# Opening of a hybrid encoder layer: the first head's fourth projection summed chunk by chunk between the modulation's weight pieces

## The chip, the cores and the metric

The kernel runs on one core of one Trainium2 chip. The metric is the device time of one execution in microseconds (us), as the median of several runs. A profiled execution gives the engines' timelines: TensorE (PE; its weight loads are PEld), VectorE (DVE), ScalarE (ACT), GpSimd (POOL), SyncE (SP, which issues most DMAs).

## The reference

One layer over two requests of 256 tokens each, model width 2048, all in float32. Only the start matters here:

```
mod = silu(c) @ ada_w + ada_b                    # 2048 x 12288
sh1, sc1, g1, sh2, sc2, g2 = split(mod, 6)
h = rmsnorm(x, mix_pre_w) * (1 + sc1) + sh1      # 512 tokens x 2048
proj = h @ w_in                                  # per head: k, q, dk, dq (4 x 128 columns), then values and gate
... 8 heads of retention and of differential attention, w_out, gate, norm
... second modulation, and a product-key expert layer (PEER) over 16384 experts
```

## The kernel before

**Arithmetic.** A float32 product is made of three fp32r matmuls over a high and a low part of each operand (`split_products`, L854 to L859: high x high, high x low, low x high). The high part of a weight block is a rounding copy by ScalarE (`split_high`, L1424), the low part the difference (GpSimd in the opening, `first_low`, L2519; VectorE in the heads, `head_low`, L2038). Below, a "product" is such a triple over one chunk of 128 rows of h.

**The opening** computes shift and scale of the first modulation and forms h, transposed, in 16 chunks of 128 x 512. The weights `ada_w` come in 32 pieces of 1 MB, four to a block of two chunks. SyncE loads them in order into a ring of five places (`ada_load`, L499; a piece waits for `ada_done` of the one that held its place). Places 3 and 4 of the ring also move: pieces 28 and 29 go to `ada_late`, because `w_fourth` lies over ring places 3 and 4 (`ada_place`, L465). TensorE takes the pieces in its loop over p (from L875): `ada_piece(p)` (L836), then at p % 4 == 3 `row_columns` (L844), which turns the block's sums into columns; ScalarE and VectorE then modulate the block's even and odd chunk, and GpSimd and VectorE make their low parts.

**Products between the pieces.** `chunk_order` (L116) writes a list by hand: the products of projections 0, 1 and 2 of head 0 over chunks 0 to 11, at most two to a step, a chunk not before step 4 * (k // 2) + 6 and a projection not before `W_READY` (its weights' split). Of the steps from 10 on, 17, 21, 25, 29, 30 and 31 hold none. After the last piece the remaining products of the three follow (chunk 13, 12, then 15 and 14 in each). Then `head_step(0, None)` runs `project(0, 3)`, the fourth, as one closed run of 16 products out of `w_fourth`, and `project(0, 4)` to `project(0, 7)`, values and gate in quarters (128x384 matmuls). Then head 1 begins with `project(1, 0)`.

**The weights of the projections** come in pieces through `w_raw`, two places in turn (`piece_load`, L508; waits until the piece two before is split). Piece 2 goes to `w_third`, piece 3 to `w_fourth`. Piece 3 is loaded after the last `ada_w` piece, split high by ScalarE after block 7, and its low part is shared: first half GpSimd, second half VectorE, which counts it on `h_odd`; the load of piece 5 waits for that.

**ScalarE's order in `head_step(0, None)`:** evacuate projections 0, 1, 2 (`evacuate`, L1444, L1453), split pieces 4 and 5, evacuate 3, split 6, 7 and 8 (8 is head 1's first), with a wait on `proj` each. **VectorE's order:** late piece 0, low part of 4, late 1, low 5, late 2 to 4, low 6, late 5 to 7, low 7, late 8 to 10, low 8, late 11. A "late piece" (`late_piece`, L2023 and L2027) is a row-wise product and sum for the later parts of the modulation, two passes over 128x1024, whose loads (`col_load`, L519) wait for a place in a ring of four. SyncE issues the loads of pieces 5 to 8 between those column loads (`head_loads`, L534).

Of the kernel before, what the change touches and what calls it, by code (L numbers as in the profile page):

```python
# [22 lines left out]
P = 128  # L23
D = 2048
KD = D // P
# [15 lines left out]
ADA_FULL = 25  # L41
# [70 lines left out]
W_READY = (7, 8, 11)  # L112
# [3 lines left out]
def chunk_order():  # L116

    queue = sorted((max(W_READY[n], 4 * (k // 2) + 6), k // 2, 1 - k % 2, n, k) for n in range(len(W_READY)) for k in range(KD - 4))
    slots = []
    for p in range(ADA_PIECES):  # L120
        slots.append([queue.pop(0)[3:] for _ in range(2) if queue and queue[0][0] <= p])
    assert not queue
    return slots


CHUNKS = chunk_order()
# [57 lines left out]
def build_program(nc, x, ct, c_rows, ada_w, ada_wt, ada_b, rows, w_t, w_v, w_o, w_q, keys_t, decay, lams, post1, pre2, post2,  # L184
# [9 lines left out]
    with ExitStack() as ctx:  # L194
# [264 lines left out]
        def ada_slot(n):  # L459
            return n % ADA_RING if n < ADA_FULL else (0, 1, 2, 3, 4, 0, 1)[n - ADA_FULL]  # L460

# [3 lines left out]
        def ada_place(n):  # L465
            return ada_late[n - ADA_FULL - 3] if n in (ADA_FULL + 3, ADA_FULL + 4) else ada_ring[ada_slot(n)]

# [24 lines left out]
        def _(sp):  # L492
# [6 lines left out]
            def ada_load(n):  # L499

                if n == ADA_FULL + 3:
                    sp.wait_ge(S["xtr"], KD)
                wait(sp, "ada_done", max([m for m in range(n) if ada_slot(m) == ada_slot(n)], default=-1) + 1)
                sp.dma_start(ada_place(n), ada_w[n]).then_inc(S[f"ada_in{ada_slot(n)}"], 16)
# [3 lines left out]
            def piece_load(h, n):  # L508

                wait(sp, "w_low", 8 * h + n - 1)  # L510
                if isinstance(h, int) and h == 0 and n == 5:
                    sp.wait_ge(S["h_odd"], BLOCKS + 1)
# [42 lines left out]
            for n in range(ADA_PIECES):  # L555
# [7 lines left out]
                if n == 8:  # L563
                    piece_load(0, 2)
                if n == LOG_PIECE:
# [3 lines left out]
            piece_load(0, 3)  # L569
            sp.wait_ge(S["silu_out"], 16)  # L570

            sp.wait_ge(S["ada_done"], ADA_FULL + 5)
# [5 lines left out]
            piece_load(0, 4)  # L578
# [246 lines left out]
        def _(pe):  # L825
# [35 lines left out]
            def chunk_product(n, k):  # L861
# [4 lines left out]
                high, low = (w_third[:, 0, c], w_third[:, 1, c]) if n == 2 else (w_high[:, n, c], w_low[:, n, c])  # L866
                last = split_products(bank(n), ((high, low), (h_hi[:, k, :], h_lo[:, k, :])), k == 1, k == KD - 2)
# [22 lines left out]
            for n, k in ((1, KD - 3), (2, KD - 3), (0, KD - 4), (1, KD - 4), (2, KD - 4)):  # L890
                chunk_product(n, k)
            for n in range(3):
# [3 lines left out]
            def project(h, n):  # L896
                wait(pe, "w_low", 8 * h + n + 1)
                r = n % 2
                place = own_place(h, n)
                high, low = (place[:, 0, :], place[:, 1, :]) if place is not None else (w_high[:, r, :], w_low[:, r, :])  # L900
                if place is not None:
                    pe.wait_ge(S["h_odd"], BLOCKS + 1)
# [90 lines left out]
            def head_step(h, a):  # L993

                def p(n):
                    if h is not None and not (a is None and n < 3):
# [392 lines left out]
        def _(act):  # L1389
# [34 lines left out]
            def split_high(h, n):  # L1424
# [4 lines left out]
                if own_place(h, n) is not None:  # L1429
                    act.wait_ge(S["xtr"], KD)  # L1430
                    if n == 3:
                        act.wait_ge(S["ada_done"], ADA_FULL)
# [11 lines left out]
            def evacuate(h, n):  # L1444
# [4 lines left out]
                if n < 4:  # L1449
# [3 lines left out]
                    acti(dst, bank(n), ACT.Copy, scale=P ** -0.5 if n == 0 else 1.0).then_inc(S["proj_ev"], 1)  # L1453
# [85 lines left out]
            for j in range(BLOCKS):  # L1539
# [5 lines left out]
                if j == 1:  # L1545
                    split_high(0, 2)
                if j == LOG_BLOCK + 1:
# [5 lines left out]
            split_high(0, 3)  # L1553
# [257 lines left out]
        def _(dve):  # L1811
# [118 lines left out]
            for j in range(1, BLOCKS):  # L1930
# [8 lines left out]
            dve.wait_ge(S["w_high"], 4)  # L1939
            vec.tensor_tensor(w_fourth[:, 1, WT // 2:], w_raw[:, 1, WT // 2:], w_fourth[:, 0, WT // 2:].bitcast(f32), ALU.subtract)\  # L1940
                .then_inc(S["h_odd"], 1)

# [106 lines left out]
            def head_step(h, a, link, last=False):  # L2049
# [22 lines left out]
                if a is None:  # L2072
                    late(0)
                    low(4)
                    late(1)
                    low(5)
                    late(2, 3, 4)
# [440 lines left out]
        def _(pool):  # L2518
            def first_low(n):  # L2519
# [3 lines left out]
                w = WT // 2 if n == 3 else WT  # L2523
                nc.gpsimd.tensor_tensor(low[:, 0:w], w_raw[:, n % 2, 0:w], high[:, 0:w].bitcast(f32), ALU.subtract)\
# [14 lines left out]
            first_low(3)  # L2539
# [181 lines left out]
```

## Time and profile before

| | us |
|---|---|
| median of 3 runs | 3203.61 (3201.92 to 3204.26) |
| the profiled execution | 3205.48 |
| its span (first to last instruction) | 3203.7 |
| TensorE matmul busy, whole span | 3139.6 |
| the last `ada_w` piece begins on TensorE | 106.87 |
| `project(0, 3)` begins, `project(0, 4)` begins | 117.63, 128.64 |
| head 1 begins | 162.42 |

In a timeline a row is: start, length, engine, line, operation, tiles written and read, shape, count of merged instructions, and in brackets the idle time before it with what ended it. A matmul's length is from its start to its modelled end, and matmuls overlap: the start of the next is what tells the pace. An issue's last number is the time until the data had landed.

### The profile page before, as it was taken

To read this page: it belongs to the slowest core of one execution; us is meant where nothing else is said; L and a number is where in the kernel's file an instruction comes from. 1 tells how busy PE (TensorE), PEld (TensorE's weight loads), DVE (VectorE), ACT (ScalarE), POOL (GpSimd) and SP (SyncE) were. 2 spreads that over 40 slices of the span, in tenths; PEclk is the share of its full clock that TensorE was granted. 3 is DMA by queue.
4 is the path that set the end of the run, shared out by engine and by line. 5 is a ranking of instruction groups with operands and counts; after the bars stand their busy time and mean duration, and the time that the engine had idled before them with its cause. 6 is when DMAs were issued, how large, how long until landed. Compare 5 with 4: busy or idle time off the path is not lost. (4 is left out here: it accounts for less than half of the span.)

```text
span 3203.7 us, 49077 instructions
## 1 busy us (share of the span) xinstructions
PE 3139.6 (98%) x19669; PEld 2984.7 (93%) x19669; DVE 2732.5 (85%) x3945; ACT 1115.8 (35%) x1457; POOL 894.6 (28%) x570
## 2 busy tenths in 40 slices
PE   7999999999999999999999999999999999999998
PEld 3788888888998888999999999999999999999998
DVE  4688888888888999979888898888688888888888
ACT  2223322333224456943333332332332332332333
POOL 2100000002445781022333233332223333333331
PEclk9999999999999999999999999999999999999999
DMA  9844444444657413899999999999799999999997
GB/s 388 322 174 165 167 168 170 162 166 172 222 184 263 158 54 122 232 332 375 376 362 378 376 379 368 366 377 357 314 374 366 357 364 360 378 362 373 369 360 299
DMA packets 175730, 929.95 MB, mean 290 GB/s; under 512 B 17025, under 2 KB 50998, under 8 KB 80310
## 3 DMA queue, kind: packets, MB, share of 16 engines
q1 hardware_dynamic: 124278, 554.01, 47.0%
q0 software_dynamic: 51264, 373.32, 30.0%
q8 instruction: 132, 2.16, 0.3%
q14 instruction: 56, 0.46, 0.0%
HBM read 891.80 MB, written 34.55 MB: 289 GB/s over the span
## 5 line engine op out<-in xcount | busy, mean ns | idle before, releaser
L1657 ACT ACTIVATE sb_raw_hi<-sb_raw_ring 128x2048 fp32r<-128x2048 f32 x256 | 491.2, 1919 | 1121.9 <-DMA sb_raw_ring<-in_v_t 574.5
L1207 PE MATMUL ps_all<-sb_h_lo,sb_raw_hi 128*128 128x336 f32 x2048 | 638.3, 319 | 0.0
L2275 DVE TENSOR_TENSOR sb_raw_lo<-sb_raw_ring,sb_raw_hi 128x2048 fp32r<-128x2048 f32 x255 | 585.1, 2295 | 52.4 <-ACT sb_raw_hi L1657 51.9
L1207 PE MATMUL ps_all<-sb_h_hi,sb_raw_hi 128*128 128x336 f32 x2016 | 628.6, 319 | 0.0
L1270 PE MATMUL ps_all<-sb_w_hi,sb_raw_hi 128*128 128x336 f32 x2032 | 623.3, 316 | 5.3 <-ACT sb_raw_hi L1657 2.2
L1271 PE MATMUL ps_all<-sb_w_lo,sb_raw_hi 128*128 128x336 f32 x2032 | 622.7, 315 | 0.0
L2637 POOL DMA_INDIRECT sb_gather_ring<-in_u_tab,sb_kept x178 | 277.3, 1558 | 758.8 <-DVE sb_kept L2419 563.8
L2637 POOL DMA_INDIRECT sb_gather_ring<-in_v_tab,sb_kept x178 | 300.7, 1689 | 609.0 <-DVE sb_acc_a L2432 384.6
L1270 PEld LDWEIGHTS ps_all<-sb_w_hi,sb_raw_hi 128*128 128x128 f32 x2032 | 382.3, 188 | 6.6 <-issue 3.8
L1207 PEld LDWEIGHTS ps_all<-sb_h_lo,sb_raw_hi 128*128 128x128 f32 x2048 | 387.3, 189 | 0.0
L1271 PEld LDWEIGHTS ps_all<-sb_w_lo,sb_raw_hi 128*128 128x128 f32 x2032 | 381.9, 188 | 0.0
L1207 PEld LDWEIGHTS ps_all<-sb_h_hi,sb_raw_hi 128*128 128x128 f32 x2016 | 380.5, 189 | 0.0
L1214 PE MATMUL ps_all<-sb_h_hi,sb_raw_lo 128*128 128x336 f32 x2016 | 337.5, 317 | 2.3 <-DVE sb_raw_lo L2275 2.3
L1284 PE MATMUL ps_all<-sb_w_hi,sb_raw_lo 128*128 128x336 f32 x2032 | 333.7, 316 | 0.0
L2419 DVE CUSTOM_DVE_ANT_0 sb_gather_ring<-sb_gather_ring,sb_arena 128x2048 f32<-128x2048 f32 x128 | 291.5, 2288 | 31.7 <-DMA sb_gather_ring<-in_u_tab,sb_kept 31.5
L2432 DVE SCALAR_TENSOR_TENSOR sb_acc_a<-sb_gather_ring,sb_kept,sb_acc_a 128x2048 f32<-128x2048 f32 x127 | 298.2, 2348 | 22.1 <-DMA sb_gather_ring<-in_v_tab,sb_kept 18.9
L1214 PEld LDWEIGHTS ps_all<-sb_h_hi,sb_raw_lo 128*128 128x128 f32 x2016 | 314.2, 188 | 2.8 <-DVE sb_raw_lo L2275 2.8
L1284 PEld LDWEIGHTS ps_all<-sb_w_hi,sb_raw_lo 128*128 128x128 f32 x2032 | 316.8, 188 | 0.0
L2546 POOL TENSOR_TENSOR sb_w_low<-sb_w_raw,sb_w_high 128x1024 fp32r<-128x1024 f32 (+1 forms) x36 | 90.8, 2545 | 746.7 <-ACT sb_w_high L1564 746.7
L1436 ACT ACTIVATE sb_w_high<-sb_w_raw 128x1536 fp32r<-128x1536 f32 (+1 forms) x62 | 105.0, 1695 | 370.4 <-PE ps_all L859 367.1
L857 PE MATMUL ps_all<-sb_h_hi,sb_w_high 128*128 128x512 f32 x480 | 192.0, 400 | 2.1 <-DVE sb_h_lo L1892 1.7
L858 PE MATMUL ps_all<-sb_h_lo,sb_w_high 128*128 128x512 f32 x480 | 187.4, 390 | 0.0
(346 smaller groups left out, 5547.5 us busy)
## 6 DMA issues: line engine op xcount, KB each, us to landing
sb_raw_ring<-in_u_t SPq DMA_DIRECT2D x128, 1024.0 KB
sb_raw_ring<-in_v_t SPq DMA_DIRECT2D x128, 1024.0 KB
sb_arena<-in_ada_wt SPq DMA_DIRECT2D x94, 512.0 KB, 6.1
sb_w_raw<-in_w_t SPq DMA_DIRECT2D x32, 1024.0 KB, 4.9
sb_small<-in_ada_w SPq DMA_DIRECT2D x30, 1024.0 KB, 10.8
sb_w_raw<-in_w_v SPq DMA_DIRECT2D x32, 768.0 KB, 4.3
sb_g_ring<-table_scratch SPq DMA_DIRECT2D x30, 672.0 KB
table_scratch<-sb_stage SPq DMA_DIRECT2D x7, 2688.0 KB, 12.3
```

Source lines behind the costliest of these rows:

```text
L857: mm(b, a_hi, b_hi, start=start, stop=False)
L858: mm(b, a_hi, b_lo, start=False, stop=False)
L1207: last = mm(acc, raw_hi[:, r[0], kk * P:(kk + 1) * P], part, start=i == 0, stop=False)
L1214: last = mm(acc, raw_lo[:, place, kk * P:(kk + 1) * P], high_of(k, kk), start=False, stop=kk == KD - 1)
L1270: mm(accs[c], v, w_hi[:, slots[e], :], start=e == 0, stop=False)
L1271: return mm(accs[c], v, w_lo[:, slots[e], :], start=False, stop=False)
L1284: last = mm(accs[c], raw_lo[:, place, e * VW + c * P:e * VW + (c + 1) * P], w_hi[:, slots[e], :], start=False, stop=e == S8 - 1)
L1657: acti(raw_hi[:, k % 2, :], raw_ring[:, k % RAW, :], ACT.Copy).then_inc(S["un_hi"], 1)
L2275: vec.tensor_tensor(raw_lo[:, k % RAW, :], raw_ring[:, k % RAW, :], raw_hi[:, k % 2, :].bitcast(f32), ALU.subtract)\
L2419: vec.tensor_tensor_reduce(out=ring, in0=ring, in1=h2a if kind == "own" else h2x[rows, :], scale=1.0, scalar=0.0, op0=ALU.mult, op1=ALU.ad ...
L2432: vec.scalar_tensor_tensor(acc, ring, hid_all[rows, c:c + 1], acc, ALU.mult, ALU.add).then_inc(S["gr_used"], 1)
L2637: pool.indirect_dma_start(out=gather_ring[:, n % GRING, :], out_offset=None, in_=u_tab if n < DOTS else v_tab, in_offset=bass.IndirectOffs ...
```

## The change

The fourth projection of head 0 is summed chunk by chunk like the other three. `chunk_order` keeps the list of the first three as it is and fills steps that hold fewer than two products with those of projection 3, from step 20 on; four are left and returned as `CHUNKS_LEFT`, and the loop after the last piece takes them and then all four projections. Projection 3 sums into bank 6 (`first_bank`), as bank 3 is used by the pieces. Its weights are loaded between pieces 14 and 15 and split in block 2, the low part by GpSimd alone; for this the pieces 13, 14, 18, 19, 23, 24, 28 and 29 go to `ada_late`. The load of piece 4 takes the old place of piece 3's. `project(0, 3)` goes. VectorE's order in head 0 begins with the low part of piece 4 and has late piece 1 behind that of piece 5.

```diff
@@ -38,7 +38,8 @@
 ADA_RING = 5
-ADA_FULL = 25
+ADA_MOVED = 13
+LAST_USES = 30
 LOG_PIECE = 16
@@ -109,21 +110,25 @@
-W_READY = (7, 8, 11)
+W_READY = (7, 8, 11, 20)
 TURNS = {3: range(0, 7), 4: range(7, 10), 5: range(10, 13), 6: range(13, KD)}
...
-    queue = sorted((max(W_READY[n], 4 * (k // 2) + 6), k // 2, 1 - k % 2, n, k) for n in range(len(W_READY)) for k in range(KD - 4))
+    rows = [sorted((max(W_READY[n], 4 * (k // 2) + 6), k // 2, 1 - k % 2, n, k) for n in ns for k in range(KD - 4)) for ns in (range(3), (3,))]
     slots = []
-    for p in range(ADA_PIECES):
-        slots.append([queue.pop(0)[3:] for _ in range(2) if queue and queue[0][0] <= p])
-    assert not queue
-    return slots
-
-
-CHUNKS = chunk_order()
+    for p in range(ADA_PIECES - 1):
+        slots.append([])
+        for _ in range(2):
+            ready = [row for row in rows if row and row[0][0] <= p]
+            if ready:
+                slots[p].append(ready[0].pop(0)[3:])
+    assert not rows[0]
+    return slots, [row[3:] for row in rows[1]]
+
+
+CHUNKS, CHUNKS_LEFT = chunk_order()
@@ -457,13 +462,16 @@
         def ada_slot(n):
-            return n % ADA_RING if n < ADA_FULL else (0, 1, 2, 3, 4, 0, 1)[n - ADA_FULL]
+            return n % ADA_RING
...
         def ada_place(n):
-            return ada_late[n - ADA_FULL - 3] if n in (ADA_FULL + 3, ADA_FULL + 4) else ada_ring[ada_slot(n)]
+            return ada_late[ada_slot(n) - 3] if n >= ADA_MOVED and ada_slot(n) >= 3 else ada_ring[ada_slot(n)]
+
+        def first_bank(n):
+            return bank(n if n < 3 else 6)
@@ -498,7 +506,7 @@
-                if n == ADA_FULL + 3:
+                if n == ADA_MOVED:
                     sp.wait_ge(S["xtr"], KD)
@@ -508,8 +516,6 @@
                 wait(sp, "w_low", 8 * h + n - 1)
-                if isinstance(h, int) and h == 0 and n == 5:
-                    sp.wait_ge(S["h_odd"], BLOCKS + 1)
                 if n < 4:
@@ -562,20 +568,21 @@
                     piece_load(0, 2)
+                if n == 14:
+                    piece_load(0, 3)
                 if n == LOG_PIECE:
...
                     sp.dma_start(iota[:, :], iota_c).then_inc(S["rows_in"], 16)
-            piece_load(0, 3)
+            piece_load(0, 4)
             sp.wait_ge(S["silu_out"], 16)
-            sp.wait_ge(S["ada_done"], ADA_FULL + 5)
+            sp.wait_ge(S["ada_done"], LAST_USES)
             sp.dma_start(dist, dist_c).then_inc(S["head_in"], 16)
...
             col_load(0, 0)
-            piece_load(0, 4)
             col_load(0, 1)
@@ -863,8 +870,9 @@
                 c = slice(k * P, (k + 1) * P)
-                high, low = (w_third[:, 0, c], w_third[:, 1, c]) if n == 2 else (w_high[:, n, c], w_low[:, n, c])
-                last = split_products(bank(n), ((high, low), (h_hi[:, k, :], h_lo[:, k, :])), k == 1, k == KD - 2)
+                place = own_place(0, n)
+                high, low = (place[:, 0, c], place[:, 1, c]) if place is not None else (w_high[:, n, c], w_low[:, n, c])
+                last = split_products(first_bank(n), ((high, low), (h_hi[:, k, :], h_lo[:, k, :])), k == 1, k == KD - 2)
                 if k == KD - 2:
@@ -887,19 +895,16 @@
             row_columns(BLOCKS - 1)
-            for n, k in ((1, KD - 3), (2, KD - 3), (0, KD - 4), (1, KD - 4), (2, KD - 4)):
+            for n, k in CHUNKS_LEFT + [(n, KD - 3) for n in range(1, 4)] + [(n, KD - 4) for n in range(4)]:
                 chunk_product(n, k)
-            for n in range(3):
+            for n in range(4):
                 chunk_product(n, KD - 1)
...
                 r = n % 2
-                place = own_place(h, n)
-                high, low = (place[:, 0, :], place[:, 1, :]) if place is not None else (w_high[:, r, :], w_low[:, r, :])
-                if place is not None:
-                    pe.wait_ge(S["h_odd"], BLOCKS + 1)
+                high, low = w_high[:, r, :], w_low[:, r, :]
                 if n < 4:
@@ -993,7 +998,7 @@
                 def p(n):
-                    if h is not None and not (a is None and n < 3):
+                    if h is not None and not (a is None and n < 4):
                         project(h, n)
@@ -1429,7 +1434,7 @@
                     if n == 3:
-                        act.wait_ge(S["ada_done"], ADA_FULL)
+                        act.wait_ge(S["ada_done"], ADA_MOVED - 3)
                     acti(own_place(h, n)[:, 0, :], w_raw[:, n % 2, :], ACT.Copy).then_inc(S["w_high"], 1)
@@ -1450,7 +1455,7 @@
                     dst = (k_t, q_t, dk_t, dq_t)[n]
-                    acti(dst, bank(n), ACT.Copy, scale=P ** -0.5 if n == 0 else 1.0).then_inc(S["proj_ev"], 1)
+                    acti(dst, first_bank(n) if isinstance(h, int) and h == 0 else bank(n), ACT.Copy, scale=P ** -0.5 if n == 0 else 1.0).then_inc(S["proj_ev"], 1)
                 else:
@@ -1544,13 +1549,14 @@
                     split_high(0, 2)
+                if j == 2:
+                    split_high(0, 3)
                 if j == LOG_BLOCK + 1:
...
                     acti(lam_dot[:, 0:2], lam_dot[:, 0:2], ACT.Exp).then_inc(S["lg_e"], 1)
-            split_high(0, 3)
             head_step(0, None)
@@ -1936,10 +1942,6 @@
                     lam_end()
-            dve.wait_ge(S["w_high"], 4)
-            vec.tensor_tensor(w_fourth[:, 1, WT // 2:], w_raw[:, 1, WT // 2:], w_fourth[:, 0, WT // 2:].bitcast(f32), ALU.subtract)\
-                .then_inc(S["h_odd"], 1)
-
             def decay_logs(a, link):
@@ -2070,11 +2072,10 @@
                 if a is None:
+                    low(4)
                     late(0)
-                    low(4)
-                    late(1)
                     low(5)
-                    late(2, 3, 4)
+                    late(1, 2, 3, 4)
                     low(6)
@@ -2520,8 +2521,7 @@
                 high, low = (place[:, 0], place[:, 1]) if place is not None else (w_high[:, n], w_low[:, n])
-                w = WT // 2 if n == 3 else WT
-                nc.gpsimd.tensor_tensor(low[:, 0:w], w_raw[:, n % 2, 0:w], high[:, 0:w].bitcast(f32), ALU.subtract)\
+                nc.gpsimd.tensor_tensor(low, w_raw[:, n % 2, :], high.bitcast(f32), ALU.subtract)\
                     .then_inc(S["w_low"], 1)
@@ -2536,7 +2536,8 @@
                     first_low(2)
-            first_low(3)
+                if j == 2:
+                    first_low(3)
```

## Rows read from the trace of the kernel before

**Rows 1.** the page, part 1: busy time, share of span, instructions
```profile
PE 3139.6 (98%) x19669; PEld 2984.7 (93%) x19669; DVE 2732.5 (85%) x3945; ACT 1115.8 (35%) x1457; POOL 894.6 (28%) x570
```

**Rows 2.** busy time by stretches: engine's us (instructions), TensorE clock, DMA share, GB/s
```profile
100.00:110.00 10.00, 8.46 (x54) 3.67 (x54) 3.91 (x10) 2.69 (x7) 1.55 (x1) 1.00 1.00 410
...
140.00:150.00 10.00, 10.00 (x60) 10.00 (x59) 9.23 (x14) 1.49 (x1) 0.00 (x0) 1.00 0.58 208
```

**Rows 3.** timeline of TensorE in the opening: start us, length us, line, tiles, count
```profile
60.26 1.06 PE L836 MATMUL ps_all<-sb_small,sb_arena 128*32 128x512 f32 x8
61.25 0.50 PE L857 MATMUL ps_all<-sb_h_hi,sb_w_third 128*128 128x512 f32 x1
...
62.83 1.06 PE L836 MATMUL ps_all<-sb_small,sb_arena 128*32 128x512 f32 x8
...
74.16 1.92 PE L836 MATMUL ps_all<-sb_small,sb_arena 128*32 128x512 f32 x16
76.02 0.50 PE L857 MATMUL ps_all<-sb_h_hi,sb_w_high 128*128 128x512 f32 x1
```

**Rows 4.** timeline of SyncE: issues of pieces 17 and 18
```profile
61.38 0.33 SPq L504 DMA_DIRECT2D sb_small<-in_ada_w  x1
...
63.96 0.33 SPq L504 DMA_DIRECT2D sb_small<-in_ada_w  x1
```

**Rows 5.** DMA issues of the same two: size, last number us to landing
```profile
sb_small<-in_ada_w SPq DMA_DIRECT2D x1, 1024.0 KB, 10.7
...
sb_small<-in_ada_w SPq DMA_DIRECT2D x1, 1024.0 KB, 10.6
```

**Rows 6.** busy time by stretches, 64 to 68 us (DMA share next to last)
```profile
64.00:68.00 4.00, 4.00 (x20) 2.08 (x20) 0.00 (x0) 0.00 (x0) 0.00 (x0) 1.00 0.50 176
```

**Rows 7.** timeline of TensorE from the last piece to the fifth projection
```profile
106.87 1.06 PE L836 MATMUL ps_all<-sb_small,sb_arena 128*32 128x512 f32 x8 [1.41 <-DMA sb_small<-in_ada_w]
...
109.57 0.48 PE L857 MATMUL ps_all<-sb_h_hi,sb_w_high 128*128 128x512 f32 x1
...
117.63 0.50 PE L857 MATMUL ps_all<-sb_h_hi,sb_w_fourth 128*128 128x512 f32 x1
...
128.64 0.33 PE L857 MATMUL ps_all<-sb_w_high,sb_h_hi 128*128 128x384 f32 x1
```

**Rows 8.** timeline of ScalarE: third projection's evacuation, fifth's split
```profile
117.76 0.60 ACT L1453 ACTIVATE sb_small<-ps_all 128x512 f32<-128x512 f32 x1 [0.76 <-PE ps_all L859]
119.46 1.49 ACT L1436 ACTIVATE sb_w_high<-sb_w_raw 128x1536 fp32r<-128x1536 f32 x1 [1.10 <-DMA sb_w_raw<-in_w_v]
```

**Rows 9.** timeline of VectorE: splits (L2041) and late pieces (L2023)
```profile
120.98 1.76 DVE L2041 TENSOR_TENSOR sb_w_low<-sb_w_raw,sb_w_high 128x1536 fp32r<-128x1536 f32 x1 [0.77 <-ACT sb_w_high L1436]
...
125.07 1.76 DVE L2041 TENSOR_TENSOR sb_w_low<-sb_w_raw,sb_w_high 128x1536 fp32r<-128x1536 f32 x1
126.74 1.22 DVE L2023 CUSTOM_DVE_ANT_0 sb_tops<-sb_arena 128x1024 f32<-128x1024 f32 x1
...
129.38 1.23 DVE L2023 CUSTOM_DVE_ANT_0 sb_tops<-sb_arena 128x1024 f32<-128x1024 f32 x1
...
157.90 2.29 DVE L2041 TENSOR_TENSOR sb_w_low<-sb_w_raw,sb_w_high 128x2048 fp32r<-128x2048 f32 x1
```

**Rows 10.** timeline of TensorE: first product of head 1
```profile
162.42 0.47 PE L857 MATMUL ps_all<-sb_h_hi,sb_w_high 128*128 128x512 f32 x1 [0.30 <-PE ps_all L859]
```

**Rows 11.** timeline of TensorE: two idle times (in brackets, us) and their ends
```profile
46.62 0.47 PE L857 MATMUL ps_all<-sb_h_hi,sb_w_high 128*128 128x512 f32 x1 [1.71 <-DVE sb_h_lo L1892]
...
809.26 2.08 PE L1075 MATMUL ps_all<-sb_w_high,sb_mix_lo 128*128 128x256 f32 x8 [2.68 <-DVE sb_mix_lo L2155]
```

**Rows 12.** busy time by stretches behind three idle times (clock: third from last)
```profile
48.00:50.00 2.00, 2.00 (x10) 1.25 (x9) 1.15 (x6) 0.91 (x3) 0.00 (x0) 0.50 0.99 406
107.00:111.00 4.00, 4.00 (x25) 2.64 (x22) 0.93 (x5) 1.29 (x4) 0.00 (x0) 1.00 1.01 418
809.00:813.00 4.00, 3.74 (x19) 3.75 (x20) 1.41 (x3) 1.91 (x1) 0.44 (x1) 0.57 0.94 328
```

## Prediction

> **What bounds the kernel now.** I read the page's first part, then the busy time in stretches of 10 us, then TensorE's timeline beside the issue and landing of each load, and last the timelines of ScalarE and VectorE behind the opening. The first says only that TensorE is busy 98% of the span [rows 1]: whatever delays TensorE at the end of the opening delays the end. The stretches show the opening with the DMA engines full (share about 1.0) and TensorE's matmul row nearly full too, but its weight loads at only 0.37; after the opening weight loads are full [rows 2]. So the question is whether the opening's TensorE has room.
>
> The step times answer it. A step with two products starts 2.57 us before the next (60.26 to 62.83), and gets to its first product after 0.99 (61.25). Pieces 17 and 18 lie in one row: 17 has no product, and from 74.16 to the first product of 18 at 76.02 are 1.86 us, so the empty step cost 0.87 [rows 3]. A row of columns adds 1.0: the last piece, one product and the row take 2.70 (106.87 to 109.57), less 1.0 and 0.7 [rows 7]. Two products in an empty step therefore cost 2.57 - 0.87 = 1.70 us, 0.85 each, against 11.01 / 16 = 0.69 each in the closed run after the opening [rows 7]: the switch between the two kinds of matmul is paid once more per filled step.
>
> The data: piece 17 is issued at 61.38 and lands 10.7 later, at 72.1; piece 18 at 63.96 plus 10.6, 74.6 [rows 4, 5]. So a MB takes 2.5 us, and both land before TensorE takes them (74.16 and about 75.05): here TensorE limits, by 2.0 and 0.5 us. Four steps hold 3 x 2.57 + 0.87 + 1.0 = 9.6 us of TensorE work against 9.9 us of loads, so the two limits run side by side, and the only visible idle time is the 1.41 us ahead of the last piece [rows 7]. The "free steps" are free of products, not of time.
>
> **What the change moves.** Worked out from the lists in the code: 48 matmuls (16 products) leave the closed run. Eight go as pairs to the steps of pieces 21, 25, 29 and 30; four stand behind the last row of columns, and the last four join the closing products.
>
> *The weight piece on the DMA queue.* Its 1 MB now goes between pieces 14 and 15, so pieces 15 to 31 land up to 2.5 us later. Between 64 and 68 the engines were only 0.50 busy, in small transfers [rows 6]: 2.0 us. The cost is between 0.5 (all of that is filled) and 2.5; I take 2.5, because piece 17 was issued at 61.4, well before 64, and still landed 2.5 ahead of piece 18, so whatever gates a landing was not short of work. The Trainium skill, "DMA: Bandwidth & Descriptors", section "Queues, rings and completion order", says that a copy is split over up to 16 engines and each takes its own ring in order; engines without small packets could then run ahead, which is the 0.5 end if it also moves the landings.
>
> *Up to the last piece.* Piece 17 lands at 74.6 instead of 72.1, so TensorE starts it 0.4 late and is through at 75.5; piece 18 lands at 77.1: 1.6 us of new idle time. From there each of the thirteen steps from piece 18 up to piece 31 holds two products, three of them a row of columns: 13 x 2.57 + 3 x 1.0 = 36.4 us. The last piece starts at 77.1 + 36.4 = 113.5 instead of 106.87 [rows 7]; its data is there by then (106.8 + 2.5 = 109.3), so the 1.41 us of waiting is gone. That is +6.6 us for 8 products.
>
> *After it.* Piece, one product and row of columns took 106.87 to 109.57, 2.7 us [rows 7]; then 19 products are left (4 + 3 + 4 + 8), 19 x 0.69 = 13.1, and 0.1 for the first: the four projections end at 129.4. Before, they ended at 128.64. The chain that made TensorE wait shortly for the last two columns of h, and 0.1 us for the fourth weights, goes: 11 products cover it.
>
> *The new wait.* The fifth projection needs its weights split, ScalarE first, VectorE second. ScalarE evacuates projections 1, 2 and 3 ahead of that split, in program order, and this is unchanged. Before, the fourth projection's 11 us lay behind the third's end and covered it all. Now the third ends two products before the fourth, at 128.0. ScalarE starts 0.2 later (the third ended near 117.6, its evacuation started at 117.76), 0.60 evacuation, 1.49 split [rows 7, 8], then VectorE at once, 1.76 [rows 9]: 128.0 + 0.2 + 0.6 + 1.5 + 1.8 = 132.1. TensorE idles 2.7 us and starts the fifth projection at 132.1 against 128.64, +3.5.
>
> *VectorE behind it.* The order is rewritten so that the fifth split comes first, and the twelve late pieces follow. Before, two late pieces and two splits were done by 126.7, under the fourth projection; now the whole queue starts at 130.35. One split is 1.67 to the next start, a late piece 2.64, or 2.41 ahead of a split [rows 9]. Up to the split that opens the next head: 4 x 1.67 + 7 x 2.64 + 4 x 2.41 + 2.29 = 37.1, so that is done at 167.45. TensorE alone would be ready at 132.1 + 33.5 = 165.6 (128.64 to 162.42 less 0.30 idle), plus 0.5 for the split of the eighth weights, 157.5 against 157.05: 166.1. It waits 1.4 us more and opens head 1 at 167.45 against 162.42 [rows 10]: **+5.0 us**. There the lag ends: the next head's first split is due after a whole projection and two rounds of scores, and 7 us later than before still makes it, by about 2 us.
>
> *At nothing:* ScalarE's split and GpSimd's full-width one move into idle time behind block 2 (the load lands before the evacuation of block 3 is due); VectorE is rid of half a split; SyncE passes the earlier load with its wait long met, and the fifth and sixth weight loads come earlier. Loads held for piece 29 come some 5 us later, and their first reader now starts at 130. The sixth to eighth loads stand behind late pieces in SyncE's order; I find them landed 1 to 4 us before use, and that is the thinnest cover here.
>
> **Clock.** After 1.71 us of idle TensorE the granted clock fell to 0.50, after 2.68 us it was 0.57 over the next four, and after 1.41 us it stayed at 1.00 [rows 7, 11, 12]. Half clock for some 3.4 us costs 1.7. The new 2.7 us idle will do it, but behind it VectorE sets the time: TensorE at 166.1 + 1.7 = 167.8 instead of 167.45, so 0.3 us at most. The 1.6 us ahead of piece 18 lies between the two rows; a fall there costs its full 1.7.
>
> **Sum.** The profiled execution took 3205.48 us at a span of 3203.7; the median shown is 3203.61, 1.9 lower. 3205.48 + 5.0 = 3210.5 profiled, or 3203.61 + 5.0 = 3208.6 as a median. A measurement tells about 0.2%, 6.4 us: slower begins at 3210.0, faster at 3197.2.
>
> **Rivals.**
> 1. *The small-transfer stretch swallows the load* (shift 0.5). Then piece 18 starts at 75.1, and everything after is 2.0 earlier: +3.0, 3206.6. For it: 2 us of idle engines. Against: landings stay 2.5 apart behind it.
> 2. *Clock or late weights on the path.* A clock fall at piece 18, or a second one, or a sixth weight load landing after 145: +6.7 or more, 3210.3 (to 3212). For it: a fall after 1.71 us. Against: none after 1.41.
> 3. *The other side: the free steps are truly idle.* If TensorE's rows there only look busy and it really waits for loads, eight products cost nothing. With the shift also swallowed the last piece starts at 107.4, the four projections end at 123.2, the fifth starts at 125.9, VectorE's queue runs 124.2 to 161.3, and head 1 opens at 161.3, -1.1: 3202.5. It decides once the shift is swallowed and the eight products cost under 3.9 us together instead of 6.8. For it: weight loads only 0.37 busy in the opening [rows 2]. The Trainium skill ("Perfetto Trace Analysis", section "Identifying the Most-Contended Engine") says matmul busy is no good measure and weight-load busy is; by that rule this is the outcome. Against: piece 17 had landed 2 us before its step, yet the full steps kept 2.57 [rows 3 to 5].
>
> **How the numbers follow.** Forecast (+5.0, with 1.5 either way for the covers) 0.53; rival 1 0.16; rival 2 0.22; rival 3 0.07; the rest 0.02. The range reaches from the upper edge of rival 3 to the top of rival 2: 3203.5 to 3212. Slower by over 0.2% is rival 2 and the edge of the forecast: 0.24; faster by so much needs what no case gives: 0.01; within 0.2%: 0.75.
>
> **What would show it.** Piece 18 starting near 77.1; the last piece near 113.5 with no idle time before it; 2.7 us of TensorE idle before the first 128x384 matmul, ended by VectorE's split; head 1's first product waiting on VectorE, near 167.4. Wrong, if pieces 21, 25, 29 and 30 with products don't lengthen by 1.7, if loads 15 to 31 are not shifted, or if head 1 opens with no wait.

## The result and the profile after

Fifteen runs of each: 3211.46 us after (3204.28 to 3215.09), 3204.26 us before (3200.89 to 3207.53). The ratio is 1.0022, 95% interval [1.0015, 1.0029], so +7.0 us (4.8 to 9.3). It lies inside the stated range (3203.5 to 3212.0), on the side that was forecast, and nearer to rival 2 (+6.7) than to the forecast (+5.0). Whether it is more than the 0.2% taken as the bound of "slower" the interval does not say. A later measurement of the same two kernels (12 and 29 runs) gave 1.0015 [1.0006, 1.0024], +4.8 us.

The profiled execution (a "profile" below) took 3214.46 us. Part 1 of its page:

```profile
PE 3139.5 (98%) x19669; PEld 2981.2 (93%) x19669; DVE 2728.6 (85%) x3944; ACT 1114.5 (35%) x1457; POOL 885.8 (28%) x570
```

The busy time by stretches of the same run (columns as in [rows 2]):

```profile
100.00:110.00 10.00, 10.00 (x59) 5.15 (x61) 6.73 (x31) 2.59 (x6) 1.02 (x1) 1.00 0.96 379
140.00:150.00 10.00, 10.00 (x60) 10.00 (x59) 9.61 (x14) 1.49 (x1) 0.00 (x0) 1.00 0.81 276
```

The sums of [rows 1] barely move. TensorE does the same matmuls and is busy for the same time (3139.5 against 3139.6 us) in a span 9.0 us longer, so what was added in sum is idle time. The opening's weight loads rose from 3.67 to 5.15 of 10 us; that looks like better use.

TensorE's timeline shows where the time went. Pieces 17 and 18 (compare [rows 3]):

```profile
74.33 1.07 PE L843 MATMUL ps_all<-sb_small,sb_arena 128*32 128x512 f32 x8 [1.06 <-DMA sb_small<-in_ada_w]
76.83 1.75 PE L843 MATMUL ps_all<-sb_arena 128*32 128x512 f32 x8 [1.43 <-DMA sb_arena<-in_ada_w]
78.51 0.80 PE L864 MATMUL ps_all<-sb_h_hi,sb_w_high 128*128 128x512 f32 x1
```

Both wait for their data, and from piece 18 on the matmuls are slow: 1.75 for a piece that took 1.07. The stretch behind shows the granted clock (third number from the end) at 0.51, half of full speed:

```profile
77.00:80.00 3.00, 3.00 (x12) 1.21 (x5) 0.00 (x0) 0.00 (x0) 0.00 (x0) 0.51 0.99 418
```

Then piece 25 with its two new products, the last piece, the first matmul of the fifth projection and the first of head 1 (compare [rows 3, 7, 10]):

```profile
98.45 1.07 PE L843 MATMUL ps_all<-sb_small,sb_arena 128*32 128x512 f32 x8
99.45 0.50 PE L864 MATMUL ps_all<-sb_h_hi,sb_w_fourth 128*128 128x512 f32 x1
...
101.03 1.07 PE L843 MATMUL ps_all<-sb_small,sb_arena 128*32 128x512 f32 x8
...
114.92 1.06 PE L843 MATMUL ps_all<-sb_small,sb_arena 128*32 128x512 f32 x8
...
133.42 0.44 PE L864 MATMUL ps_all<-sb_w_high,sb_h_hi 128*128 128x384 f32 x1 [2.60 <-DVE sb_w_low L2043]
...
168.78 0.50 PE L864 MATMUL ps_all<-sb_h_hi,sb_w_high 128*128 128x512 f32 x1 [1.30 <-DVE sb_w_low L2043]
```

The last piece no longer waits, but it starts 8.05 us later than before, with only eight products fewer behind it. Two new waits on VectorE's splits follow, 2.60 and 1.30. Head 1 opens 6.4 us later than in [rows 10]. ScalarE and VectorE in between (compare [rows 8, 9]):

```profile
129.50 0.60 ACT L1458 ACTIVATE sb_small<-ps_all 128x512 f32<-128x512 f32 x1 [0.76 <-PE ps_all L866]
129.99 2.85 ACT L1441 ACTIVATE sb_w_high<-sb_w_raw 128x1536 fp32r<-128x1536 f32 x2
```

```profile
131.60 1.76 DVE L2043 TENSOR_TENSOR sb_w_low<-sb_w_raw,sb_w_high 128x1536 fp32r<-128x1536 f32 x1 [10.83 <-ACT sb_w_high L1441]
133.28 1.22 DVE L2025 CUSTOM_DVE_ANT_0 sb_tops<-sb_small,sb_arena 128x1024 f32<-128x1024 f32 x1
```

The third evacuation, ScalarE's splits, VectorE's split: the chain of the prediction, with VectorE idle for 10.83 us ahead of it, where two late pieces used to run.

The profile is 9.0 us over that of before, 2.6 more than at head 1. The extra lies far behind, at one matmul of the expert layer, whose longest wait nearby was 1.44 before:

```profile
2229.99 0.39 PE L1275 MATMUL ps_all<-sb_w_hi,sb_raw_hi 128*128 128x336 f32 x1 [3.87 <-DVE sb_y_t L2409]
```

A second profile of the same kernel (below) opened head 1 4.2 us later than before and ended 4.9 later, so the extra of the first is not seen to come with the change. Single times of one kernel spread over some 10 us here, and an interval is some 3 us to each side. The experiments are therefore read from the traces, from the start of piece 18 on. Ahead of it the profiles differ by up to 5 us (piece 18 starts between 74.95 and 79.96), in part through falls of the clock early in the opening. Most kernels have one profile, so that a difference of some tenths of a us between two kernels shows little.

### The profile page after: what moved, and what is told of

It is laid out like the page before. It is cut to its first block and busy times, and to the rows that moved or that the text cites. A ratio compares the mean times of both kernels' runs of the same rounds, so it can differ in the third digit from the quotient of the medians.

```text
span 3212.7 us, 49090 instructions
## 1 busy us (share of the span) xinstructions
PE 3139.5 (98%) x19669; PEld 2981.2 (93%) x19669; DVE 2728.6 (85%) x3944; ACT 1114.5 (35%) x1457; POOL 885.8 (28%) x570
## 5 line engine op out<-in xcount | busy, mean ns | idle before, releaser
L2638 POOL DMA_INDIRECT sb_gather_ring<-in_v_tab,sb_kept x178 | 284.7, 1600 | 622.2 <-DVE sb_acc_a L2433 391.6
L866 PE MATMUL ps_all<-sb_h_hi,sb_w_low 128*128 128x512 f32 x480 | 187.4, 390 | 0.0
```

The costliest lines, as they stand in the source:

```text
L866: return mm(b, a_lo, b_hi, start=False, stop=stop)
L2638: pool.indirect_dma_start(out=gather_ring[:, n % GRING, :], out_offset=None, in_=u_tab if n < DOTS else v_tab, in_offset=bass.IndirectOffs ...
```

## The experiments

Theory: the moved megabyte makes TensorE wait at pieces 17 and 18; products in steps cost nearly what they save; the orders on ScalarE and VectorE make the two later waits; a fall of the clock at piece 18 adds 1.7. Rivals: the steps are free; the load is swallowed; the later waits are for data.

**The load cut to 64 KB**, in the changed kernel. Only one chunk of the fourth projection's weights is loaded; its other chunks are computed from what lies in the buffer, so that its results mean nothing and only its time is of use.

```diff
+                if isinstance(h, int) and h == 0 and n == 3:
+                    sp.dma_start(w_raw[:, 1, 0:P], w_t[0, 3, :, 0, :]).then_inc(S["w_in1"], 16)
+                elif n < 4:
```

> The changed kernel, but the early load of piece 3 brings 64 KB (one chunk of its weights) in place of 1 MB; the fourth projection's other chunks are computed from what is left in that buffer. Theory (the 1 MB shifts pieces 15 to 31 by 2.2 to 2.5 us, makes TensorE idle ahead of pieces 17 and 18, and that idle time lets the clock fall): piece 17 lands near 71.9, piece 18 starts near 74.4, no fall of the clock there, the last piece starts near 110.8 instead of 114.9, the fifth projection near 129.4 instead of 133.4, head 1 near 164.8 instead of 168.8: about -4 us against the changed kernel, +2.4 against the kernel before. Rival (the load is swallowed, the products alone cost the time): the last piece stays near 114.9 and head 1 near 168.8.

Pieces 17 and 18:

```profile
72.60 1.06 PE L845 MATMUL ps_all<-sb_small,sb_arena 128*32 128x512 f32 x8 [0.76 <-DMA sb_small<-in_ada_w]
75.08 1.90 PE L845 MATMUL ps_all<-sb_arena 128*32 128x512 f32 x8 [1.42 <-DMA sb_arena<-in_ada_w]
```

Half a miss. Pieces 17 and 18 landed within 0.7 us of what was expected (72.6 and 75.0), and piece 18 starts 1.75 earlier than in the changed kernel, but the waits stay and the clock falls all the same. TensorE started piece 16 at 69.19, against 71.58 in the profile of before and 70.62 in that of the change, and met the data's limit without the megabyte. The last piece started at 113.25 (expected 110.8), head 1 at 167.18 (expected 164.8). 3210.18 us, ratio 1.0014 [1.0004, 1.0024]. So the idle time ahead of piece 18 is not the load's alone. The kernel before stands at that edge too: in the profile of it TensorE was late, as its clock had been at half from 27.4 to 34.4 and from 48.0 to 51.4 us [rows 12], but its variant with products in fours (below), the same program up to piece 22, waited as well:

```profile
72.47 1.06 PE L838 MATMUL ps_all<-sb_small,sb_arena 128*32 128x512 f32 x8 [0.28 <-DMA sb_small<-in_ada_w]
74.95 1.06 PE L838 MATMUL ps_all<-sb_small,sb_arena 128*32 128x512 f32 x8 [1.42 <-DMA sb_small<-in_ada_w]
```

**The load alone, on the kernel before.** The load, the places and the split as in the change; `project(0, 3)` stays.

```diff
+                if n == 14:
+                    piece_load(0, 3)
...
-            piece_load(0, 3)
+            piece_load(0, 4)
```

> The kernel before, with the load of piece 3, the places of the modulation's pieces and the split of the fourth weights moved as in the change; the fourth projection stays one closed run and VectorE's order stays. Theory: pieces 17 to 31 land 2.2 to 2.5 us later, the last one starts on TensorE near 109.2 instead of 106.9 (a fall of the clock at piece 18 is absorbed, as TensorE waits for data again at pieces 22, 26 and 31), the fourth projection starts near 119.8, the fifth near 130.8 with no idle time before it, head 1 near 164.7: +2.3 against the kernel before. Rival (shift swallowed by the stretch of small transfers): head 1 near 162.4 and the time unchanged.

Pieces 17 and 18 waited 1.89 and 1.41, the clock fell to 0.52 for the next 7 us, the last piece started at 110.5, with its data, and head 1 opened:

```profile
165.76 0.47 PE L857 MATMUL ps_all<-sb_h_hi,sb_w_high 128*128 128x512 f32 x1 [0.30 <-PE ps_all L859]
```

That is +3.3 (expected +2.3) with no wait for VectorE. The late start of piece 18 (2.9) reached the end of the opening. The fall did so only in part: the two steps from piece 18 on took 8.96 us against 6.12 before, but from piece 18 to the last piece it is 32.5 against 31.8, as the rest took the place of waits that the profile of before has there. 3206.02 us, 1.0004 [0.9995, 1.0014]: the times do not tell +3.3 from nothing. The landings do: without the megabyte piece 17 landed at 72.1, 72.4 and 72.6 (before, its variant in fours, the 64 KB load), in the ten profiles with it and with the small loads on SyncE at 73.6 to 77.4, 75.1 in the middle. So the load is not swallowed; how much of it reaches head 1 differs from profile to profile.

**No fourth-projection product in the steps.**

```diff
-W_READY = (7, 8, 11, 20)
+W_READY = (7, 8, 11, ADA_PIECES)
```

> The changed kernel with no product of the fourth projection in the steps: its first twelve all follow the last piece. Theory (a pair in a step costs 1.70 us of TensorE, in the closed run 1.38, and the steps without products then wait for data): the last piece starts near 109.2, the four projections end near 130.6 (109.2 + 2.7 + 27 x 0.69 + 0.1), the fifth starts near 133.2 after 2.6 us idle, head 1 near 168.5: within 0.5 us of the changed kernel. Rival (the steps hide the eight products): the four projections end 5.5 us later than in the changed kernel, near 136.3, head 1 near 174.

```profile
109.46 1.07 PE L843 MATMUL ps_all<-sb_small,sb_arena 128*32 128x512 f32 x8 [1.43 <-DMA sb_small<-in_ada_w]
...
133.38 0.44 PE L864 MATMUL ps_all<-sb_w_high,sb_h_hi 128*128 128x384 f32 x1 [2.59 <-DVE sb_w_low L2043]
...
168.81 0.47 PE L864 MATMUL ps_all<-sb_h_hi,sb_w_high 128*128 128x512 f32 x1 [0.30 <-DVE sb_w_low L2043]
```

A hit to 0.3 us: without the eight products the last piece waits for data again, at 109.46, and head 1 opens at the same time as in the first profile of the changed kernel, which had a fall at piece 18 where this one has none. Against the second profile of the changed kernel, without that fall (below), from piece 18 to the end of the four projections it is 53.6 us instead of 52.4: the eight products, 5.5 us in the closed run, save 1.2 when put into the steps. 3209.92 us, 1.0020 [1.0010, 1.0030]. This is the run against rival 3, by which they would save all 5.5.

**From step 17 on.**

```diff
-W_READY = (7, 8, 11, 20)
+W_READY = (7, 8, 11, 17)
```

> The changed kernel with the fourth projection allowed from step 17 on (its weights are split by 70.3 us, step 17 starts at 74.3): two products fill step 17, ten in all stand in steps. Theory: they take the place of the idle time ahead of piece 18, so that the clock does not fall there; piece 18 starts near 76.9, the last piece near 113.3 instead of 114.9, the four projections end near 127.8 instead of 130.8, the fifth starts near 130.5 (still 2.6 us idle), head 1 near 165.9: -2.9 us against the changed kernel. Rival (the fall comes from the 1.06 us idle ahead of piece 17 or from the phase of the window): the clock still falls and head 1 is near 167.6.

Piece 18 started at 77.75 with no wait, no fall; the last piece at 114.33, 36.6 behind it; head 1 at 166.86, after a 1.30 us wait for VectorE. From piece 18 to head 1 89.1 us instead of 91.95, or 90.5 in the second profile of the changed kernel. 3208.31 us, 1.0013 [1.0004, 1.0023]. As expected, but for a later start (piece 17 landed 0.8 later in this profile). That the products kept the clock up is not shown: it had fallen earlier here (0.50 between 30 and 32 us), and no profile with such an early fall has one at piece 18 (last section).

**ScalarE's order.** `split(4)` behind the first evacuation, `split(5)` behind the second, in head 0 alone.

```diff
                 p(0)
+                if a is None:
+                    split(4)
...
                 p(1)
+                if a is None:
+                    split(5)
```

> The changed kernel with ScalarE splitting the fifth weights straight after it has evacuated the first projection, and the sixth after the second, instead of after the third. Theory (the 2.6 us of TensorE idle ahead of the fifth projection are the chain evacuation, split, second split behind the third projection's end): the fifth projection starts with the end of the fourth, near 130.9 instead of 133.4; VectorE's queue starts near 129.0, so that head 1 opens near 166.1 and still waits for VectorE, about 1.7 us: -2.7 us against the changed kernel. Rival (the wait is for data or for head_in, not for the order): idle time of 2.6 us stays, head 1 near 168.8.

```profile
130.48 0.44 PE L864 MATMUL ps_all<-sb_w_high,sb_h_hi 128*128 128x384 f32 x1
...
165.87 0.50 PE L864 MATMUL ps_all<-sb_h_hi,sb_w_high 128*128 128x512 f32 x1 [1.29 <-DVE sb_w_low L2046]
```

The idle time ahead of the fifth projection is gone, the wait for VectorE at head 1 stays: the first wait was ScalarE's order. From piece 18 to head 1 it is 87.8 us, 2.7 less than in the second profile of the changed kernel. 3210.13 us, 1.0022 [1.0013, 1.0032]: this gain does not show in the times.

**VectorE's order.** Late pieces 0 and 1 ahead of the fifth split.

```diff
-                    low(4)
                     late(0)
+                    late(1)
+                    low(4)
                     low(5)
-                    late(1, 2, 3, 4)
+                    late(2, 3, 4)
```

> The changed kernel with VectorE's first two late pieces ahead of the fifth weights' second split, two late pieces less behind it. Theory (VectorE's queue of 37 us behind that split makes head 1 wait 1.3 us): the fifth projection starts as in the changed kernel, near 133.4, VectorE is done with the split for head 1 near 163.7, and head 1 opens without waiting for it, near 167.2: -1.6 us. Rival (VectorE's order does not bound): head 1 near 168.8, or later if the two late pieces delay the split.

```profile
134.19 0.44 PE L864 MATMUL ps_all<-sb_w_high,sb_h_hi 128*128 128x384 f32 x1 [2.49 <-DVE sb_w_low L2043]
...
169.61 0.47 PE L864 MATMUL ps_all<-sb_h_hi,sb_w_high 128*128 128x512 f32 x1 [0.30 <-PE ps_all L866]
```

```profile
135.00:139.00 4.00, 4.00 (x16) 4.00 (x16) 3.82 (x6) 0.00 (x0) 0.00 (x0) 0.57 0.96 348
```

The wait for VectorE at head 1 is gone, but no time with it: the clock fell behind the 2.49 us of idle time (0.57 over four us), and 35.4 us passed from the fifth projection to head 1, as in the changed kernel. With VectorE's queue as the limit such a fall was covered (133.2 to 136.6 in the run with the 64 KB load, 35.4 us as well); with the queue shortened TensorE bears it. 3210.90 us, 1.0023 [1.0013, 1.0032].

**Both orders.** The two diffs above together.

> Both orders together, the rest as in the changed kernel. Theory: fifth projection near 130.9, head 1 near 164.6 with no wait for VectorE: -4.2 us against the changed kernel, about +2.2 against the kernel before, which is what the moved load costs. Rival (the two waits overlap and only one can be won): -2.7 us.

Fifth projection straight behind the fourth, head 1 without a wait for VectorE; 33.8 us from one to the other, as before. From piece 18 to head 1 86.1 us, 4.3 less than in the second profile of the changed kernel: the two waits add up (2.7 and 1.6). 3205.87 us, 1.0006 [0.9997, 1.0015].

**Both orders and step 17.**

> Both orders and the fourth projection from step 17 on. Theory: no fall of the clock at piece 18, four projections end near 127.8, the fifth starts near 127.9, head 1 near 161.6: -7.2 us against the changed kernel and -0.8 against the kernel before (162.4), so same as before within the noise of a measurement. Rival (the moved megabyte costs its 2.3 us whatever the order): head 1 near 164.

```profile
73.80 1.07 PE L843 MATMUL ps_all<-sb_small,sb_arena 128*32 128x512 f32 x8 [1.56 <-DMA sb_small<-in_ada_w]
76.39 1.06 PE L843 MATMUL ps_all<-sb_arena 128*32 128x512 f32 x8
...
161.29 0.47 PE L864 MATMUL ps_all<-sb_h_hi,sb_w_high 128*128 128x512 f32 x1 [0.30 <-PE ps_all L866]
```

A hit at head 1 (161.6 expected): 7.5 and 5.4 us less than in the two profiles of the changed kernel and 1.1 less than before. 3203.34 us, 0.9998 [0.9989, 1.0007]: the change's whole cost is taken back, and nothing that can be measured is won. Here too the clock had fallen early (0.61 between 30 and 32 us), so what step 17 does to the clock stays open.

**The changed kernel again.**

> The changed kernel itself once more, for a second look at its opening. Of six looks so far at kernels with a megabyte moved or products in later steps, the clock fell at piece 18 where TensorE's idle times ahead of pieces 17 and 18 came to 2.2 us or more, and not where they came to 1.9 or less, though the one ahead of 18 was 1.4 in all. Theory: the same here, and the last piece starts 38.1 us behind piece 18 with a fall, 36.5 without; head 1 opens 37.9 us behind the end of piece 31's start plus 15.9, so 53.9 us behind it. Time: +7 us against the kernel before.

```profile
73.69 1.07 PE L843 MATMUL ps_all<-sb_small,sb_arena 128*32 128x512 f32 x8 [0.94 <-DMA sb_small<-in_ada_w]
76.17 1.06 PE L843 MATMUL ps_all<-sb_arena 128*32 128x512 f32 x8 [1.42 <-DMA sb_arena<-in_ada_w]
...
131.20 0.44 PE L864 MATMUL ps_all<-sb_w_high,sb_h_hi 128*128 128x384 f32 x1 [2.60 <-DVE sb_w_low L2043]
...
166.65 0.47 PE L864 MATMUL ps_all<-sb_h_hi,sb_w_high 128*128 128x512 f32 x1 [0.30 <-DVE sb_w_low L2043]
```

```profile
76.00:80.00 4.00, 3.83 (x23) 1.62 (x24) 0.00 (x0) 0.11 (x1) 0.00 (x0) 1.00 1.01 426
131.00:137.00 6.00, 5.80 (x24) 5.80 (x25) 5.93 (x9) 0.11 (x1) 0.00 (x0) 0.72 0.38 134
```

My rule on the sum of two idle times falls: 0.94 + 1.42 is 2.36, and the clock stayed. This time it fell behind the 2.60 us, where VectorE covers it. 3209.98 us, 1.0015 [1.0006, 1.0024], +4.8 us (1.9 to 7.7) where +7 was expected.

**Products in fours**, on the kernel with both orders and step 17, then on the kernel before.

```diff
+for _p in range(22, 30, 2):
+    CHUNKS[_p + 1], CHUNKS[_p] = CHUNKS[_p] + CHUNKS[_p + 1], []
```

> The kernel with both orders and the fourth projection from step 17 on, and the products of steps 22, 24, 26 and 28 put behind piece 23, 25, 27 and 29, four in a row there. Theory (a switch between a piece's matmuls and the products costs 0.33 us per filled step, and TensorE is behind its data there): four switches less, 1.3 us, of which up to 0.3 goes into waiting for pieces 23 to 29; the last piece starts 35.5 us behind piece 18 instead of 36.6, head 1 opens 1.1 us earlier relative to piece 18: 3203.3 - 1.1 = 3202.2, about 2 us under the kernel before, too little to be told from no change. Rival (the price is in the products, not in the switch): 36.6 us as before, or more, as the products wait for the second piece.

On the first: from piece 18 to the last piece 35.2 us (79.39 to 114.56) instead of 36.6, 1.4 less where four switches were priced at 1.3. The last piece's data had landed at 111.1. Head 1 opened at 162.76, 83.4 behind piece 18; that is 1.5 less than in the ungrouped kernel, though piece 18 started 3 us later in this profile. 3205.85 us, 0.9999 [0.9989, 1.0010].

> The kernel before with the same grouping of its products. Theory (there the last piece waits for its data, so TensorE's price of the steps is not what counts): the saved 1.3 us turn into idle time ahead of pieces 23 to 31, the last piece starts with its data, near 106.9, head 1 near 162.4, time unchanged. Rival (TensorE bounds the opening before as well): about -1.3 us.

```profile
87.37 1.06 PE L838 MATMUL ps_all<-sb_small,sb_arena 128*32 128x512 f32 x8 [1.40 <-DMA sb_small<-in_ada_w]
107.21 0.64 PE L838 MATMUL ps_all<-sb_small,sb_arena 128*32 128x512 f32 x4 [0.44 <-DMA sb_small<-in_ada_w]
```

Idle time at piece 23, and the last piece still waits for its data; head 1 at 162.75. 3203.34 us, 1.0000 [0.9990, 1.0009]. The kernel before is bound by its data at the last piece, the changed one by TensorE.

**The small loads from another queue**, on the kernel with both orders and step 17.

```diff
                     split_high(0, 2)
+                    act.dma_start(lg_all, decay.partition_broadcast(P)).then_inc(S["rows_in"], 16)
+                    act.dma_start(lam_in, lams.partition_broadcast(P)).then_inc(S["rows_in"], 16)
+                    act.dma_start(iota[:, :], iota_c).then_inc(S["rows_in"], 16)
```

> The kernel with both orders and the fourth projection from step 17 on, and the three small loads (decay, lambdas, iota) issued by ScalarE behind block 1 instead of by SyncE behind piece 16. Before and after alike, pieces 16 and 17 land 5.2 to 6.5 us apart where 2.5 is the rule, with the DMA engines half busy between. Theory (the small loads stand in SyncE's order in front of piece 17 and half empty the engines; from another queue they run beside the big ones): pieces 16 and 17 land 2.5 us apart, piece 17 lands 2 to 3 us earlier relative to piece 16, TensorE no longer idles ahead of it, and head 1 opens about 1.5 us earlier than with the small loads on SyncE (161.3), near 159.8: 3201.8, at or a little under the kernel before. Rival (the small loads cost the same 3.5 us of the engines wherever they are issued): pieces 8 to 16 land later by that, piece 17 at the same time, no gain.

The small loads ran between 54 and 64 us, beside pieces 12 to 14. DMA share (next to last) in the middle of that:

```profile
56.00:60.00 4.00, 4.00 (x27) 2.32 (x24) 1.72 (x7) 2.08 (x5) 1.29 (x1) 1.00 0.93 367
```

and where they stood between pieces 16 and 17 in SyncE's queue:

```profile
66.00:70.00 4.00, 3.99 (x26) 2.18 (x30) 0.90 (x1) 0.78 (x2) 4.00 (x1) 1.00 0.54 214
```

The theory of the queue holds: 0.93 instead of 0.54, and pieces 16 and 17 land 2.5 us apart instead of 5.3 (4.7 to 6.7 in the thirteen other profiles). The rival is right in part: pieces 13 to 16 landed 1.3 to 1.5 us later, so 17 came 1.4 sooner and not 2.8. The last piece's data came 2.4 sooner, 1.0 of which arose only behind piece 18. The loads were also issued some 5 us earlier than before, so queue and time of issue were changed together. The gain did not follow: TensorE now waited 0.95 ahead of piece 15 instead of 0.60 there and 1.56 ahead of piece 17, and from there its own work sets the time. Head 1 at 161.04, 0.25 less (1.5 expected). 3203.68 us, 0.9997 [0.9988, 1.0006].

## Why the prediction held, point by point

| | forecast | first profile | second profile |
|---|---|---|---|
| piece 18 starts | 77.1 | 76.83 | 76.17 |
| idle ahead of 17, of 18 | 0.4, 1.6 | 1.06, 1.43 | 0.94, 1.42 |
| last piece starts | 113.5 | 114.92 | 112.70 |
| idle, fifth projection starts | 2.7, 132.1 | 2.60, 133.42 | 2.60, 131.20 |
| idle ahead of head 1 | 1.4 | 1.30 | 0.30 (clock fell, covered) |
| head 1 opens | 167.45 | 168.78 | 166.65 |

- *Price of a pair in a step.* 98.45 to 101.03 is 2.58 for a step that took 0.87 when empty: 1.7, as worked out, and thirteen steps took 36.5 us in the second profile (36.4 in the sum). The runs with no product in steps and with fours confirm it from both sides. Rival 3 is out. The Trainium skill's rule ("Perfetto Trace Analysis", section "Identifying the Most-Contended Engine"), that TensorE's headroom is judged by MFU (the matmul work as a share of the peak) or weight-load busy and not by matmul busy, misleads here if it is read by weight-load busy: at 3.67 of 10 us there was room for a gain of 1.2 us by eight products that take 5.5. What shows it is the distance from start to start.
- *The load.* 2.5 was the better end: piece 17 landed 2.2 and 1.5 us later than before in the two profiles of the change, and 3.0 later in the middle of the ten. Small transfers did not swallow it, and with the load alone the delay reached head 1. Why they leave the engines half idle the last run shows, as far as queue and time of issue can be told apart: they stood in one queue with the pieces. The Trainium skill, "DMA: Bandwidth & Descriptors", section "Queues, rings and completion order", says that SyncE and ScalarE have a ring each on every DMA engine and that an engine takes turns between them; the share of 0.93 in this run agrees.
- *ScalarE's wait and VectorE's queue.* Both as forecast to 0.1 us in the first profile, and the runs with each order changed take away just the one and the other.
- *"Behind it VectorE sets the time"*, so that a fall of the clock there costs nothing: from the fifth projection to head 1 it is 35.4 us in three profiles with a fall and in two without, and the counter-case with VectorE's queue shortened shows the price. That the 2.7 us idle "will do it" was too firm: behind 2.5 to 2.6 us the clock fell in four profiles of six, and in the first profile of the change it did not.
- *"1.6 us of new idle time" at piece 18* was not all new. The sum took TensorE as late as in one profile of before (piece 18 ready at about 75.05, data at 74.6). The other profile with before's order of loads idled 0.28 and 1.42 there and started piece 18 at 74.95, so the delay that came out, 1.2 to 1.9 (76.17 and 76.83), is the landing's and fits the 2.05 of the sum.
- *What was mis-sized: the clock at piece 18.* I priced it rightly (36.5 without, 38.1 with: 1.6 us) but gave it, with two others, a chance of 0.22. It fell in four of the seven profiles in which TensorE idled 1.4 us ahead of piece 18 and 0.2 us or more ahead of 17, with the changed order of loads or the 64 KB load. "None after 1.41" was one sight. I had also put the idle time ahead of 17 at 0.4, from a profile in which earlier falls had held TensorE back. The falls alone do not explain the first median: +5.0 without and +6.7 with one would mix to some +6, and it came out at +7.0, the second at +4.8, with intervals of 4.5 and 5.8 us. So the times bear out the sum but can't tell it from rival 2, and how often the clock fell in the unprofiled runs is not known.
- *"Within 0.2%" at 0.75* was too sure for a forecast of 0.16% with a known unknown of 1.7 us upwards.

## What to carry to other kernels

An engine that shares a stage with a full DMA queue may have idle steps in its list and no idle time: measure from start to start, with and without the work, and compare with the landings, before filling "free" steps. Work that runs long at the end of a stage often covers a chain on other engines; when it is moved, the orders behind it have to move too, here ScalarE's split ahead of its evacuations and VectorE's late pieces back under the projections. Small loads in a queue of large ones can half empty the DMA engines, but making them cheaper gains only if data is what is late next. And one profile can show room or a wait that the next does not: a forecast of a few us wants two profiles of the kernel before.

## What was not expected of the hardware

- The granted clock fell behind the same 1.4 us of idle time in some profiles and not in others. Idle ahead of pieces 17 and 18: 1.06 and 1.43, 0.76 and 1.42, 1.89 and 1.41, 1.68 and 1.42 with a fall; 0.94 and 1.42, 0.42 and 1.43, 0.28 and 1.42, 0.20 and 1.41 without. The larger sums fell, but 2.36 did not and 2.18 did. What does part them in these profiles is the clock's past: the four with a fall at piece 18 are the four of all fourteen profiles in which the clock was at 1.00 from the start up to there. In the other ten it was at 0.50 to 0.61 between 30 and 32 us, and none of them fell at piece 18. The first profile of the change, then the second:

```profile
0.00:75.00 75.00, 51.03 (x295) 24.95 (x295) 35.27 (x78) 23.19 (x33) 24.31 (x12) 1.00 0.94 387
```

```profile
30.00:34.00 4.00, 3.50 (x16) 2.90 (x16) 2.87 (x5) 3.42 (x4) 1.28 (x1) 0.57 1.00 418
```

Why that is so is open.
- The same holds of longer idle times: all fourteen profiles idle 1.71 us ahead of a first product at 45 to 48 us, as in [rows 11], and the clock fell behind it in six of them; behind the 2.5 to 2.6 us ahead of the fifth projection in four of six.
- Falls early in the opening and the wait for data cancel in part. In the eight profiles without a fall between 48 and 56 us TensorE was ready for piece 17 at 71.8 to 73.6 us, in the six with one at 74.2 to 77.1; seven of the eight then waited there for data. So part of what such a fall costs is hidden where data is late next.
- Three small loads of 200 KB in all took up 2.2 to 4.2 us between two landings when issued in the pieces' queue (4.7 to 6.7 us apart instead of 2.5), and delayed the pieces by about 1.5 from a second queue.
